# RG-LRU projections: seven products of half blocks in place of two full projections, with the weight sums made a block ahead

## The reference, cut to what matters

```
u = h @ Wu[:, block j]        # 1024 x 128
g = h @ Wy[:, block j]        # 1024 x 128
u = centred_conv4(u) + bias
for d in (forward, backward):
    r = sigmoid(u @ wa[d][j] + ba);  i = sigmoid(u @ wx[d][j] + bx)
    a = exp(-8 * softplus(-lambda) * r)
    h_d = scan(h_d * a + sqrt(1 - a*a) * i * u)
out[block j] = gelu(g) * (h_fwd + h_bwd)
```

## Time and profile before

| | |
|---|---|
| median of 3 runs | 3610.54 us (3609.0 to 3611.76) |
| the profiled execution | 3606.29 us, span 3604.5 us |
| TensorE busy | 3485.2 us, 97% of the span |
| VectorE, ScalarE, GpSimd busy | 53%, 32%, 26% |
| mean granted TensorE clock | 0.993 |
| the RG-LRU's rounds | from 2220.58 us to 2434.63 us by TensorE |

### The profile page before, as it was taken

One profiled execution on the slowest core, in us unless ns is written; L12 is line 12 of the kernel. 1 busy time (PEld: TensorE's weight loads), 2 busy tenths in 40 slices (PEclk: granted clock), 3 DMA queues, 4 the chain that ended last, 5 costly groups with the idle time before them and its releaser, 6 DMA issues.

```text
span 3604.5 us, 53981 instructions
## 1 busy us (share of the span) xinstructions
PE 3485.2 (97%) x22362; PEld 2340.3 (65%) x22362; DVE 1900.5 (53%) x3554; ACT 1142.9 (32%) x2161; POOL 919.6 (26%) x736
## 2 busy tenths in 40 slices
PE   8999999999999999999999999999999999999998
PEld 4555555655667977777777756444455545878887
DVE  3555553355445354666666653455777732554543
ACT  3444443222232022333333322764544521110100
POOL 2212221222210003555555410223445420000000
PEclk9999999999999999999999999999999999999999
DMA  5112111101012121111111111221101011222221
GB/s 227 65 71 79 51 64 53 35 35 47 28 43 106 58 78 59 48 44 42 47 48 48 54 71 59 83 76 62 48 31 48 17 68 62 108 84 80 86 81 56
DMA packets 29555, 229.78 MB, mean 64 GB/s; under 512 B 3072, under 2 KB 6784, under 8 KB 9728
## 3 DMA queue, kind: packets, MB, share of 16 engines
q1 hardware_dynamic: 29312, 226.33, 16.9%
HBM read 224.22 MB, written 2.10 MB: 63 GB/s over the span
## 4 chain that ended last, share of the span: by engine, by line
PE 88%; DVE 6%; ACT 3%; issue 2%; DMA 1%; POOL 1%; SPq 0%; DVEq 0%; ACTq 0%; POOLq 0%
PE bank L1295 12%; PE bank L1608 11%; PE bank L1514 7%; PE bank L1950 7%; PE bank L1602 4%; PE bank L1977 4%; PE bank L1729 3%; PE bank L1868 2%; PE bank L1420 2%; PE bank L1688 2%; PE bank L1695 2%; PE bank L1453 2%; PE bank L1242 2%; PE bank L1914 2%; PE bank L1866 1%
## 5 line engine op out<-in xcount | busy, mean ns | idle before, releaser
L1295 PE MATMUL bank<-xT,ring 128*128 128x384 f32 x896 | 323.6, 494 | 2.3 <-ACT Y L2092 2.2
L3612 POOL TENSOR_TENSOR ring<-ring 128x512 f32<-128x512 f32 x112 | 146.8, 1327 | 412.6 <-DMA ring<-in_w 410.8
L3650 POOL TENSOR_TENSOR ring<-ring 128x512 f32<-128x512 f32 x128 | 171.5, 1346 | 285.0 <-DMA ring<-in_w 284.2
L1295 PE MATMUL bank<-hT,ring 128*128 128x384 f32 x672 | 242.8, 493 | 0.1
L1608 PE MATMUL bank<-Y,ring 128*128 128x384 f32 (+1 forms) x768 | 240.7, 457 | 0.0
L1295 PEld LDWEIGHTS bank<-xT,ring 128*128 128x128 f32 x896 | 161.3, 190 | 108.1 <-issue 15.7
L3676 POOL TENSOR_TENSOR arena<-arena 128x512 f32<-128x512 f32 x112 | 184.0, 1643 | 170.8 <-PE bank L1658 155.4
L1608 PE MATMUL bank<-hT,ring 128*128 128x384 f32 (+1 forms) x576 | 184.8, 457 | 9.2 <-DVE arena L3047 8.5
L1729 PE MATMUL bank<-hT,ring 128*128 128x512 f32 x384 | 178.9, 600 | 4.7 <-ACT Y L2067 4.7
L1608 PEld LDWEIGHTS bank<-Y,ring 128*128 128x128 f32 x768 | 141.2, 190 | 64.7
L1295 PEld LDWEIGHTS bank<-hT,ring 128*128 128x128 f32 x672 | 121.4, 190 | 80.9 <-issue 16.0
(11 more groups left out here) (588 smaller groups left out, 7509.8 us busy)
## 6 DMA issues: line engine op xcount, KB each, us to landing
ring<-in_w SPq DMA_DIRECT2D x77, 1024.0 KB, 4.7
ring<-in_w SPq DMA_DIRECT2D x35, 2048.0 KB, 8.5
ring<-in_w SPq DMA_DIRECT2D x20, 1280.0 KB, 5.6
ring<-in_w SPq DMA_DIRECT2D x10, 1536.0 KB, 7.3
ring<-in_w SPq DMA_DIRECT2D x8, 1408.0 KB, 5.9
ring<-in_w SPq DMA_DIRECT2D x6, 512.0 KB, 3.5
xT<-in_xT SPq DMA_DIRECT2D x1, 3072.0 KB, 14.5
xT<-in_xT SPq DMA_DIRECT2D x4, 512.0 KB, 6.5
```

Of the source, the lines that this page charges most:

```text
L1295: ins = e.matmul(bank[spot["st", kind, n, at]][:, 0:384], left[:, k], right[:, k], start=first and k == 0, stop=k == 3, skip_group_check=True)
L3612: e.tensor_tensor(s[:, i], l, r, op).then_inc(up("st_s", (kind, n, i)), 1)
L3650: e.tensor_tensor(s[:, i], l, r, op).then_inc(up("gs_s", (kind, n, i)), 1)
```

## The change

`rg_steps` is written anew. For the blocks 1 to 11 the two projections u and g, seen as a 2 x 2 product (two output tiles, two halves of the 1024 inputs, two halves of the 512 tokens), are made by seven products of half blocks, each of four matmuls of 128 x 128 by 128 x 256, in three banks. Block 0 keeps the old form.

- Four sums of token halves (`rp_t`, VectorE, 128 x 1024 each) are made once, and four sums of weight halves (`rp_s`, GpSimd, 128 x 512 each) for every block, in the round before it is used. They need that block's slab, and the product of the block now running that has read the sum's place.
- Seven results (`rp_r`, VectorE, two copies and five additions of 128 x 256 from PSUM) put the products together, u straight into the padded tile, g into `yr`. ScalarE's copy of u goes, and its gelu reads `yr` in place of the bank.
- The round is now: products 0 to 3 of block n, gate products of block n-1 (`rg_k`), `rg_a` of n-1, VectorE's `rg_h` of n-2, product 4, three weight sums of block n+1, GpSimd's part of `rg_h` of n-2 (now `rg_o`), products 5 and 6, the convolution of n (`rg_c`), the fourth weight sum, GpSimd's part of `rg_a` of n-1 (now `rg_x`), and what `RG_SIDE` has for the round. Before, a block's scans came three rounds behind its first product, now two.
- `work` goes round five banks instead of six. `RG_SIDE` is unchanged.

```
 def rg_steps():
-    jobs = ([[("rg_u", j)], [("rg_g", j)], [("rg_a", j)], [("rg_h", j)]] for j in range(12))
-    return [s for n, g in enumerate(pipeline(jobs)) for s in g + RG_SIDE.get(n, [])]
+    made = [("rp_t", i) for i in range(4)] + [("rg_u", 0), ("rg_c", 0), ("rg_y", 0)] + [("rp_s", 1, i) for i in (2, 0, 1, 3)]
+    for n in range(1, 14):
+        pair = n < 12
+        for p in range(4):
+            made += [("rp", n, p), ("rp_r", n, p)] * pair
+        made += [("rg_k", n - 1), ("rg_a", n - 1)] * (n < 13) + [("rg_h", n - 2)] * (n > 1)
+        made += [("rp", n, 4), ("rp_r", n, 4)] * pair + [("rp_s", n + 1, i) for i in (2, 0, 1)] * (n < 11)
+        made += [("rg_o", n - 2)] * (n > 1) + [("rp", n, 5), ("rp_r", n, 5), ("rp", n, 6), ("rp_r", n, 6), ("rg_c", n)] * pair
+        made += [("rp_s", n + 1, 3)] * (n < 11) + [("rg_x", n - 1)] * (n < 13) + RG_SIDE.get(n, [])
+    return made
...
+        rp_T = [Y_[:, 6144 + 1024 * n:7168 + 1024 * n].rearrange("p (k t) -> p k t", k=4) for n in range(4)]
+        rp_S = [[xT[:, 2 * n + k // 2, LAT + 128 * (k % 2):LAT + 128 * (k % 2) + 128] for k in range(4)] for n in range(4)]
...
             def rg_lam():
-                work.cells[:] = [2, 3, 5, 6, 7, 4]
+                work.cells[:] = [3, 5, 6, 7, 4]
...
+            def rp(j, p):                                   # TensorE
+                if p == 0:
+                    slab("rg", 20)
...
+                    pair_banks.reverse()
+                    take(0, ("rp", j, 0), ("rp_v", (j, 3)))
+                if p == 1:
+                    take(pair_banks[0], ("rp", j, 1), ("rp_v", (j, 6)))
+                if p == 2:
+                    take(pair_banks[1], ("rp", j, 2), ("rp_v", (j, 5)))
...
+                at, left, right = ((0, [w[:, 2 * k + 1, :] for k in range(4)], hT[:, 0:4, 0:256]),
+                                   (1, rp_S[1], rp_T[1]), (2, rp_S[2], rp_T[2]),
+                                   (0, [w[:, 2 * k + 1, :] for k in range(4, 8)], hT[:, 4:8, 0:256]),
+                                   (1, rp_S[0], rp_T[0]), (2, [w[:, 2 * k, :] for k in range(4, 8)], rp_T[3]),
+                                   (1, rp_S[3], hT[:, 4:8, 256:512]))[p]
+                if p in (1, 2, 4, 6):
+                    q.wait_ge(*on("rp_s", (j, {1: 1, 2: 2, 4: 0, 6: 3}[p])))
+                if p in (1, 2, 4, 5):
+                    q.wait_ge(*on("rp_t", {1: 1, 2: 2, 4: 0, 5: 3}[p]))
+                if p >= 3:
+                    q.wait_ge(*on("rp_v", (j, {3: 0, 4: 1, 5: 2, 6: 4}[p])))
+                m = bank[spot["rp", j, at]][:, 0:256]
+                for k in range(4):
+                    ins = e.matmul(m, left[k], right[:, k], start=p in (0, 1, 2, 4) and k == 0, stop=k == 3,
+                                   skip_group_check=True)
...
+            def rp_r(j, p):                                 # VectorE
...
+                q.wait_ge(*on("rp_mm", (j, p)))
...
+                if p in (0, 3):
+                    e.tensor_copy(first1, m).then_inc(up("rp_v", (j, p)), 1)
+                    return
...
+                e.tensor_tensor(o, m, other, ALU.add).then_inc(up("rp_v", (j, p)), 1)
...
+            def rp_s(j, n):                                 # GpSimd
+                i = spot["rp_slab", j]
+                q.wait_ge(*on(f"w{slot_of(i)}", i))
...
+                if j > 1:
+                    q.wait_ge(*on("rp_mm", (j - 1, (4, 1, 2, 6)[n])))
...
+                e.tensor_tensor(rp_sum(n), l, r, op).then_inc(up("rp_s", (j, n)), 1)
```

More of the change, by code:

```diff
@@ L962, in build, with rp_tile, rp_sum, rp_half @@
         rg_pad, rg_us, rg_gt = cells(3, 516), cells(4, 512), cells(12, 512)
+        rp_T = [Y_[:, 6144 + 1024 * n:7168 + 1024 * n].rearrange("p (k t) -> p k t", k=4) for n in range(4)]
+        rp_S = [[xT[:, 2 * n + k // 2, LAT + 128 * (k % 2):LAT + 128 * (k % 2) + 128] for k in range(4)] for n in range(4)]
+        def rp_tile(j, t):
+            o = rg_pad[j % 3][:, 2:514] if t else yr[:, j, :]
+            return o[:, 0:256], o[:, 256:512]
+        def rp_sum(n):
+            return xT[:, 2 * n:2 * n + 2, LAT:ALL].rearrange("p a (b c) -> p a b c", b=2)
+        def rp_half(i, tile, high):
+            w = slab_place(i, 2560)[:, 0:2048].rearrange("p (h a b n c) -> p h a b n c", h=2, a=2, b=2, n=2)
+            return w[:, high, :, :, 1 - tile, :]
         at[0], spare[0] = 9788, 10240
@@ L1987, in tensor @@
                   "gl_u": gl_u, "gl_d1": gl_d1, "gl_m": gl_m, "gl_o": gl_o, "gl_n": gl_n, "rg_lam": rg_lam,
-                  "rg_u": rg_u_, "rg_g": rg_g, "dn_gate": dn_gate, "dn_p": dn_p, "dn_nm": dn_nm, "dn_t": dn_t,
+                  "rg_u": rg_u_, "rg_y": rg_y, "rp": rp, "rg_k": rg_k, "dn_gate": dn_gate, "dn_p": dn_p, "dn_nm": dn_nm, "dn_t": dn_t,
                   "dn_cols": dn_cols, "dn_k": dn_k, "dn_g": dn_g, "dn_z": dn_z, "dn_l0": dn_l0, "dn_l1": dn_l1,
@@ L2347, in rg_u, with rg_k @@
                 e.activation(rg_pad[j % 3][:, 2:514], bank[spot["rg_u", j]], ACT.Copy).then_inc(up("rg_padded", j), 1)
-            def rg_g(j):
-                q.wait_ge(*on("rg_y_mm", j))
-                e.activation(yr[:, j, :], bank[spot["rg_y", j]], ACT.Gelu_apprx_tanh).then_inc(up("rg_gelu", j), 1)
+            def rg_k(j):
+                q.wait_ge(*(on("rp_v", (j, 6)) if j else on("rg_y_mm", j)))
+                e.activation(yr[:, j, :], yr[:, j, :] if j else bank[spot["rg_y", j]],
+                             ACT.Gelu_apprx_tanh).then_inc(up("rg_gelu", j), 1)
                 for g in range(4):
@@ L2565, in scalar @@
                   "gl_o": gl_o,
-                  "gl_n": gl_n, "rg_lam": rg_lam, "rg_u": rg_u, "rg_g": rg_g, "rg_a": rg_a, "dn_gate": dn_gate, "dn_gate2": dn_gate2,
+                  "gl_n": gl_n, "rg_lam": rg_lam, "rg_u": rg_u, "rg_k": rg_k, "rg_a": rg_a, "dn_gate": dn_gate, "dn_gate2": dn_gate2,
                   "dn_c": dn_c, "dn_cs": dn_cs, "dn_sq": dn_sq, "dn_nr": dn_nr, "dn_t": dn_t, "dn_cols": dn_cols, "dn_gc": dn_gc,
@@ L3151, in rg_lam, with rp_t, rg_c @@
                 e.tensor_scalar(spl[:, 0:24], spl[:, 0:24], 4.0, None, ALU.mult).then_inc(up("lam"), 1)
-            def rg_u(j):
+            def rp_t(n):
+                lo, hi = ([hT[:, k:k + 4, t:t + 256] for t in (0, 256)] for k in (0, 4))
+                for k in range(8):
+                    q.wait_ge(*on(*h_tile(2, 0, k)))
+                if n in (1, 3):
+                    q.wait_ge(*on("rp_t", n // 2))
+                l, r = ((lo[1], lo[0]), (hi[1], rp_T[0]), (hi[1], lo[1]), (hi[0], rp_T[1]))[n]
+                e.tensor_tensor(rp_T[n], l, r, ALU.subtract).then_inc(up("rp_t", n), 1)
+            def rp_r(j, p):
+                m = bank[spot["rp", j, (0, 1, 2, 0, 1, 2, 1)[p]]][:, 0:256]
+                (first1, first2), (second1, second2) = rp_tile(j, 0), rp_tile(j, 1)
+                q.wait_ge(*on("rp_mm", (j, p)))
+                if p in (1, 2, 4, 5):
+                    q.wait_ge(*on("rp_v", (j, {1: 0, 2: 1, 4: 2, 5: 4}[p])))
+                if p == 2:
+                    q.wait_ge(*(on("rg_conv", (j - 3, 3)) if j >= 3 else on("rg_zero", j)))
+                if p in (0, 3):
+                    e.tensor_copy(first1, m).then_inc(up("rp_v", (j, p)), 1)
+                    return
+                o, other = {1: (first2, first1), 2: (second2, first2), 4: (second2, second2),
+                            5: (second1, first2), 6: (first2, first2)}[p]
+                e.tensor_tensor(o, m, other, ALU.add).then_inc(up("rp_v", (j, p)), 1)
+            def rg_c(j):
                 o, c = rg_us[j % 4], rg_pad[j % 3]
-                q.wait_ge(*on("rg_padded", j))
+                q.wait_ge(*(on("rp_v", (j, 5)) if j else on("rg_padded", j)))
                 if j >= 4:
@@ L3579, in vector @@
                   "gl_i": gl_i, "gl_c": gl_c, "gl_u": gl_u, "gl_d2": gl_d2, "gl_x": gl_x, "gl_a": gl_a,
-                  "gl_y": gl_y, "rg_lam": rg_lam, "rg_u": rg_u, "rg_h": rg_h, "dn_gate": dn_gate, "dn_gate1": dn_gate1,
+                  "gl_y": gl_y, "rg_lam": rg_lam, "rp_t": rp_t, "rp_r": rp_r, "rg_c": rg_c, "rg_h": rg_h, "dn_gate": dn_gate, "dn_gate1": dn_gate1,
                   "dn_c": dn_c, "dn_nd": dn_nd, "dn_cols": dn_cols, "dn_e": dn_e, "dn_m": dn_m, "dn_pk": dn_pk,
@@ L3682, in rg_lam, with rg_x @@
                     e.memset(rg_pad[n], 0.0).then_inc(up("rg_zero", n), 1)
-            def rg_a(j):
+            def rp_s(j, n):
+                i = spot["rp_slab", j]
+                q.wait_ge(*on(f"w{slot_of(i)}", i))
+                if n in (1, 3):
+                    q.wait_ge(*on("rp_s", (j, n // 2)))
+                if j > 1:
+                    q.wait_ge(*on("rp_mm", (j - 1, (4, 1, 2, 6)[n])))
+                g, u = ([rp_half(i, tile, high) for high in range(2)] for tile in range(2))
+                l, r, op = ((u[0], u[1], ALU.add), (rp_sum(0), g[0], ALU.subtract), (g[0], u[0], ALU.subtract),
+                            (g[1], rp_sum(1), ALU.subtract))[n]
```

(2 more changed lines are left out.)

20 lines of the change are left out of this document (13 added, 7 removed).

## The result

The changed kernel takes **3624.3 us** (median of six runs, 3622.5 to 3626.7), the kernel before 3610.1 (3608.3 to 3611.8): a ratio of 1.0043 [1.0033, 1.0053], **14.2 us slower**. The forecast was 3616.7 in a range of 3600 to 3627. (The profiled executions are single runs, of 3626.7 and 3606.3 us, and differ by more than the medians do.)

What follows compares the result with a forecast made beforehand. TensorE was taken as the bound, busy 97% of the span. Terms -18.3 + 7.2 + 1.5 + 4 + 8 + 1.3 + 2.5 = +6.2 us on 3610.5 gave 3616.7 us, range 3600 to 3627.

Steps and rivals of the forecast that it cites:

- TensorE's work: u and g of 11 blocks: seven products take 12.07 us a block instead of 13.74, -18.3 us.
- Regular rounds: Rounds 3, 4, 8 to 11: VectorE and GpSimd take turns, so each runs 1.2 us over 15.5, +7.2 us.
- the walk: One round followed instruction by instruction: product 0's result queues behind the convolution, so product 3 starts at 6.0, not 5.2.
- Bank behind `dn_gate`: Round 5: block 5's first product waits for ScalarE to read the projection's bank 0, +1.5 us (0 to 1.6).
- Slab 6: Round 6: the slab lands late and three weight sums must follow before product 1, +4 us (2.7 to 6).
- `dn_gate1`: Round 7: its six VectorE instructions delay product 0's result, so product 3 waits, +8 us (3.8 to 9).
- The end: Block 11's gates wait for its convolution, +3.3, less the 2.04 us output wait: +1.3 us (-0.5 to 3).
- The clock: Behind the waits of 8, 4 and 3.3 us TensorE may run at a lower clock, +2.5 us (0 to 7).
- second rival: Strict VectorE-GpSimd turns set the rounds at 17.5 us: +14.2 us, 3625 us; chance 0.20.
- point of decision: For strict turns: a round above 17.17 us, where the change gives nothing back.
- third rival: Special rounds' waits overlap with backlog, rounds 16.7 us in all cases: some -11 us, 3599 us; chance 0.05.
- count of turns: Convolution, scans and all GpSimd work add up one after another, so a round needs 16.3 to 17 us.

Runs made afterwards that it cites:

- e2: Changed kernel without the weight sums of blocks 2 to 11, leaving out that part of the computation: 3606.6 us, 0.9995 of the kernel before.
- e9: Changed kernel without the fourth weight sum in blocks 2 to 11, leaving out that part of the computation: 3620.3 us, 1.0035 of the kernel before.
- e6: Changed kernel with GpSimd's two gate products made by VectorE, behind the result of product 4: 3617.0 us, 1.0024 of the kernel before.
- e10: Changed kernel with GpSimd's gate products waiting for the convolution and the fourth weight sum behind them: 3620.7 us, 1.0033 of the kernel before.
- e11: e5 with the edit of e10 on top: 3640.6 us, 1.0089 of the kernel before.
- e5: Changed kernel with the moves of e1, e3 and e4 together: 3601.4 us, 0.998 of the kernel before.
- e3: Changed kernel with `dn_gate` ahead of block 0 and `dn_gate1` in round 1: 3608.4 us, 1.0001 of the kernel before.
- e4: Changed kernel with the first two steps of the next stage's projection ahead of block 11's gate products: 3615.6 us, 1.0024 of the kernel before.
- e8: Kernel before with four more GpSimd products a round in blocks 0 to 9, on data nobody reads: 3616.5 us, 1.0018 of the kernel before.
- e1: Changed kernel with the result of product 0 ahead of the convolution in VectorE's queue: 3623.8 us, 1.0045 of the kernel before.

## Why the prediction was right in its places and short in its sum

The forecast was +6.2 us, and +14.2 came: the direction and the places were right, the size was under half. The steps, as forecast and as found:

- TensorE's work, -18.3: right. A round free of waits is 15.52 us (e2).
- Regular rounds, +7.2: mis-sized, **+10.2**. The wait is where it was put, before product 3, ended by the copy of product 0's result, and the walk gave 0.8 us for 1.17. Seven rounds have it, not six (round 2 too), and each costs 1.46 us: the idle time of 1.17 and some 0.3 of restart (0.16 us of overlap with the matmuls before it is lost, and the next matmuls start 1.83 us behind it instead of 1.73).
- Bank behind `dn_gate`, +1.5: right (1.48). Slab 6, +4: 3.2, right within its bounds; the transfer itself was only 0.3 of it, the sums behind it 2.5. `dn_gate1`, +8: 9.1. The end, +1.3: the gates' wait cost 3.8 for 3.3, and the 2.04 us of the earlier trace rows went as forecast, for the output was in at 2471.97 and its reader came at 2476.65.
- The clock, +2.5: mis-sized, **+5.5** in three places of the profiled execution. I had taken less than one fall like that of the earlier trace rows and kept the others in the range; each of the three waits of 2.5 us and more was followed by one, of 1.6 to 2.1 us.

The two terms that were too small make up 6 of the 8 us between forecast and medians: 3.0 for the clock and 3.0 for the regular rounds, half of that for a seventh round with the wait and half for taking 1.2 us a round where it was 1.46. The other terms were off by up to 1.1 us, in both directions. With all of them as measured the sum is +13.0; the last 1.2 us to the medians are in no term. The total fell on the number of the second rival (3625), even to its +14.2, but that is luck and not its mechanism: it put the rounds at 17.5 us and the point of decision at 17.17, and they are 16.97. The third rival's sum was wrong as worked out: eleven rounds at 16.7 give 11 x 0.47 = -5.2 us, not -11; nothing else rested on it.

Of the **reasons** that I gave for the regular rounds, the walk through VectorE's queue held and the count of turns did not. I took the sum of all turns, 16.3 to 17 us, as what a round needs, and 16.97 looks like proof. It isn't: GpSimd idles for 5.3 us of such a round and VectorE for 3.8, the round stays the same with one turn less (e9), falls by 0.1 us where the count falls by 1.1 (e6), and it gets longer when the turns are only rearranged (e10, e11). What the runs show in its place is two chains on VectorE, each with its own slack. Convolution, result 0, product 3 and gates is one: undisturbed, the copy would be done 1.4 us before product 3 is due, and the convolution grows by 2.75. Scans, result 4, product 6 is the other, and its slack is smaller: in the changed kernel the result is in at 2390.59 + 0.40 = 2390.99, and product 6 is due two products behind 2388.33, at 2391.8, so 0.8 us are left. GpSimd's eight instructions have to lie beside the one or the other, or in the idle time that their own waits (product 4 has read the sum's place) forbid them. The changed kernel happens to keep its scans clear, and pays 1.2 us at the convolution. e5 pays 0.9 there. No order that was tried pays nothing, and whether one exists, with a second place for the sum that product 4 reads, so that its successor need not wait for product 4, was not tried.

On the rule that I had weighed (the Trainium skill, "SBUF — State Buffer", Who interferes with whom: the port pair that VectorE shares with GpSimd is an exclusive lock; its words on the whole instruction stand there for VectorE's 2-port modes, and I had applied them to instructions with two SBUF inputs), pairs of a convolution step and a GpSimd instruction take 5.00 / 3 = 1.67 us, where 0.75 + 1.26 one after another make 2.01. The exclusion is real, but by 0.34 us a pair less than full, as in the earlier trace rows.

## What to carry to other kernels

When one engine's work is cut by moving some to two engines that hold each other up, don't add up their busy times: take every instruction of theirs that the bound engine waits for, see what lies in front of it in its queue, stretch that by the neighbour's instructions that run at that time, and compare it with its own slack. Then price each stop of TensorE with the restart and the lower clock behind it, not with its idle time alone. And look at what stands irregularly between rounds (here two gate steps, a slab and the last block): it cost more than the regular rounds did, and moving the two gate steps away (e3) was worth 15 to 16 us, more than any other order inside a round.

## What the hardware showed that I had not expected

- A tensor-scalar of VectorE with a single SBUF tensor was held up beside GpSimd: the convolution's first step, 0.54 us alone, took 1.48 us beside two weight sums.

```profile
2330.02 1.48 DVE L3241 TENSOR_SCALAR arena<-arena,cols 128x512 f32<-128x512 f32 x1
2329.95 2.67 POOL L3776 TENSOR_TENSOR xT<-ring 128x512 f32<-128x512 f32 x2 [10.75 <-DMA ring<-in_w]
```

- A scan, which was never disturbed in the kernel before (1224 to 1227 ns), isn't immune: 2.18 us in e10, a mean of 2001 ns in e11.
- In these runs the granted clock's lower level followed every long wait and most short ones. In the rounds and up to 2480 us, e11 left aside, the profiled runs hold 8 waits of TensorE of 5 to 9 us, all followed by slow records, and 20 of 2 to 4 us, of which 15 were: the five that were not lasted 2.04 (the kernel before), 2.53 (e4), 2.83 (e5), 3.24 (e6) and 3.54 us (e8), while one of 2.19 (e1) was. Behind one and the same wait of 2.32 us at the stage's start 16 records took 7.1 us in two profiled runs and 8.8 in the twelve others. The Trainium skill ("TensorE: Matmul & The Clock Gate", Part 1) says of a kernel's start that the number of slow matmuls varies from run to run for the same kernel; the traces show the same behind this wait, and a single profile can't price it.
